# Layer 2's down projection as seven block products of half-size operands

## The reference, cut to what matters

```
D_MODEL, SEQ, D_FF, CONV_W = 1024, 512, 2816, 3
v = rmsnorm(h, norm_ffn_w[l])
gate = causal_depthwise_conv_2(v @ w_gate[l], conv_w[l], conv_b[l])
h = h + (jax.nn.silu(gate) * (v @ w_up[l])) @ w_down[l]
...
return rmsnorm(h, final_norm_w)
```

## Time and profile before

| what | value |
|---|---|
| time, median of 3 runs | 1179.99 us (1179.94 to 1180.92) |
| the profiled execution | 1179.95 us, its span 1178.2 us |
| granted clock of the matrix engine, mean | 0.997 |
| matrix engine busy | 1149.7 us (98%) |
| VectorE, ScalarE, GpSimd busy | 827.9, 628.5, 619.5 us |

### The profile page before, as it was taken

The page is one execution under the profiler, slowest core; times in us unless marked ns, Lnnn a source line. Parts: engine busy times, 40 slices in busy tenths (PEclk is TensorE's granted clock), DMA queues, the critical chain, the costliest instruction groups (busy, mean ns, idle before and its releaser), DMA issues.

```text
span 1178.2 us, 19195 instructions
## 1 busy us (share of the span) xinstructions
PE 1149.7 (98%) x7668; PEld 995.2 (84%) x7668; DVE 827.9 (70%) x1095; ACT 628.5 (53%) x1007; POOL 619.5 (53%) x316
## 2 busy tenths in 40 slices
PE   7999999989999999999999999999999999999997
PEld 6877767779999999888877777778799999998886
DVE  5998974388888887544665577943868888875444
ACT  6346585545666565322455646656556565653323
POOL 3651132696767675544783210018867675755443
PEclk9999999999999999999999999999999999999999
DMA  5688771735866767636432211213245354442221
GB/s 185 236 224 220 191 210 19 187 105 199 202 205 200 200 217 216 196 130 159 118 109 80 72 37 38 74 36 108 74 123 145 110 148 121 144 142 81 100 90 72
DMA packets 110786, 162.64 MB, mean 138 GB/s; under 512 B 3587, under 2 KB 90986, under 8 KB 110698
## 3 DMA queue, kind: packets, MB, share of 16 engines
q1 hardware_dynamic: 97738, 115.02, 30.7%
q0 software_dynamic: 12800, 46.14, 15.9%
q10 hardware_dynamic: 160, 0.26, 0.1%
HBM read 159.05 MB, written 48.23 MB: 176 GB/s over the span
## 4 chain that ended last, share of the span: by engine, by line
PE 86%; DVE 6%; POOL 3%; ACT 3%; issue 1%; DMA 0%; POOLq 0%; ACTq 0%; DVEq 0%
PE ps L2374 34%; PE ps L2425 10%; PE ps L2429 10%; PE ps L2040 6%; PE ps L2041 6%; PE ps L2042 6%; PE ps L2129 4%; PE ps L2613 4%; PE ps L2175 1%; POOL htmp L717 1%; PE ps L2565 1%; PE ps L2160 1%; POOL w_lo L662 1%; DVE diag L1395 1%; DVE act_t L1585 1%
## 5 line engine op out<-in xcount | busy, mean ns | idle before, releaser
L662 POOL TENSOR_TENSOR w_lo<-w_raw,w_hi 128x1024 fp32r<-128x1024 f32 x176 | 458.9, 2624 | 246.5 <-ACT w_hi L806 245.1
L806 ACT ACTIVATE w_hi<-w_raw 128x1024 fp32r<-128x1024 f32 x210 | 220.9, 1054 | 198.3 <-PE ps L2429 77.2
L2374 PE MATMUL ps<-tt,w_hi 128*128 128x256 f32 x1280 | 232.4, 283 | 0.5 <-DVE w_lo L1368 0.3
L2374 PEld LDWEIGHTS ps<-tt,w_hi 128*128 128x128 f32 x1280 | 199.6, 192 | 0.9 <-DVE w_lo L1368 0.5
L2374 PE MATMUL ps<-tt,w_lo 128*128 128x256 f32 x640 | 181.1, 283 | 0.0
L1614 DVE TENSOR_TENSOR tt<-act_t,tt 128x512 fp32r<-128x512 f32 x44 | 99.1, 2259 | 101.7 <-ACT tt L1033 101.7
L2040 PE MATMUL ps<-h_hi,w_hi 128*128 128x512 f32 x376 | 153.0, 407 | 2.4 <-POOL w_lo L662 0.8
L2041 PE MATMUL ps<-h_lo,w_hi 128*128 128x512 f32 x376 | 147.0, 391 | 0.0
L2042 PE MATMUL ps<-h_hi,w_lo 128*128 128x512 f32 x376 | 146.8, 391 | 0.0
L2374 PE MATMUL ps<-h_hi,w_hi 128*128 128x256 f32 x440 | 124.6, 283 | 0.2 <-POOL w_lo L662 0.2
L2374 PE MATMUL ps<-h_lo,w_hi 128*128 128x256 f32 x440 | 124.5, 283 | 0.0
(11 more groups left out here) (334 smaller groups left out, 2284.8 us busy)
## 6 DMA issues: line engine op xcount, KB each, us to landing
blocks<-in_w_up POOLq DMA_DIRECT2D x28, 1408.0 KB, 10.5
w_raw<-in_w_up SPq DMA_DIRECT2D x40, 512.0 KB, 3.6
w_raw<-blocks SPq DMA_DIRECT2D x40, 512.0 KB, 4.0
w_raw<-in_w_in SPq DMA_DIRECT2D x19, 1024.0 KB, 5.4
w_raw<-in_w_down SPq DMA_DIRECT2D x18, 1024.0 KB, 5.0
w_raw<-in_w_gate SPq DMA_DIRECT2D x20, 512.0 KB, 3.7
w_raw<-in_w_out SPq DMA_DIRECT2D x8, 1024.0 KB, 5.2
blocks<-in_w_gate POOLq DMA_DIRECT2D x4, 1408.0 KB, 7.3
```

The costliest lines, as they stand in the source:

```text
L662: pool.tensor_tensor(unit_view(w_lo, at, flat), unit_raw(at, flat), unit_view(w_hi, at, flat).bitcast(F32), ALU.subtract).then_inc(s_lo, 1)
L806: act.activation(unit_view(w_hi, at, flat), unit_raw(at, flat), ACT.Copy).then_inc(s_hi, 1)
L2374: mm = pe.matmul(ps[:, bank, 0:NH], weight[:, k, n], a, start=begin, stop=False, skip_group_check=True)
```

## The change

The activation (transposed, inner dimension by tokens) is cut into 2 x 2 blocks of 1408 x 256, and `w_down_2` into blocks of 1408 x 512. Seven products of sums of blocks take the place of eight products of blocks. A product is a phase (`PHASES = 7`): 11 slices k of 128 rows, two token tiles, three matmuls. A phase has six units (`PHASE_UNITS = 6`): five of 128x1024 (two slices of 512 columns) and one of 128x512. There are now 42 units, and each is loaded on its own.

- **Weights.** Two phases read `w_down_2` alone, four read sums from the new DRAM tensor `dsums`, one reads `w_down_2` again. GpSimd issues 16 more DMAs (`down_sums`): eight copies and eight that add, 704x512 values each (four of the copies are within `dsums`), six during layer 2's input projection and ten in its up projection.
- **Low parts of weights.** From the fifth unit on, VectorE makes four of the six of a phase, GpSimd the first and the fourth.
- **Activation.** The sums of activation blocks (`operand_sum`) are made by VectorE in place in `act_t`, for phases 2, 3, 5 and 6, one step ahead. `operand_hi` and `operand_lo` split each operand, one phase ahead of its use.
- **Results.** Phases 3, 4 and 5 add to what a bank already holds. VectorE adds or subtracts the two banks of a finished phase to the residual in the first two steps of the next phase (`added`).
- **The end.** Token tiles finish in the order 2, 3, 0, 1, and the last phase runs its last three slices tile by tile.

The core of the diff:

```diff
+PHASES, PHASE_UNITS = 7, 6
+U_END = U_DOWN2 + PHASES * PHASE_UNITS
+D_ROW, D_CROSS, D_SUM = (2, 3), (4, 5), (0, 1)
+PHASE_BANK = (D_ROW, D_CROSS, D_SUM, D_ROW, D_SUM, D_ROW, D_CROSS)
+PHASE_FREE = {3: 1, 4: 5, 5: 7, 6: 3}
+TILE_ORDER = (2, 3, 0, 1)
...
 def on_vector(u):
     at = block_of(u)
+    if u >= U_DOWN2 + 4:
+        return (u - U_DOWN2) % PHASE_UNITS not in (0, 3)
...
+SUMS_AFTER |= {u: 1 for u in range(U_IN2 + 5, U_IN2 + 17, 2)}
+SUMS_AFTER |= {u: 1 for u in range(FIRST_BLOCK[1], U_DOWN2, NB)}
...
+            def phases():
+
+                w, k1, k2 = w_down_2[0], slice(0, KP * P), slice(KP * P, DFF)
+                left, right = slice(0, DK), slice(DK, DM)
+                streams = (w[k1, left], w[k2, left], dsums[0], dsums[1], dsums[3], dsums[2], w[k2, right])
+                for p, block in enumerate(streams):
+                    if 2 <= p < 6:
+                        sp.wait_ge(s_prep, 16 * (2 * STEPS + 4 * (p - 1)))
+                    for q in range(PHASE_UNITS):
+                        one_block(U_DOWN2 + PHASE_UNITS * p + q, block[2 * q * P:min(2 * q + 2, KP) * P, :])
...
+            def down_sums(step):
...
+                pool.wait_ge(s_prep, 16 * (2 * STEPS + step))
+                if kind == 0:
+                    pool.dma_start(dsums[to, r, :], begin).then_inc(s_prep, 16)
+                else:
+                    pool.dma_start(dsums[to, r, :], added, accum_op=ALU.add).then_inc(s_prep, 16)
...
+            def phases():
+
+                operand_hi(0, 4)
+                operand_hi(0, 5)
+                for s in range(PHASES * PHASE_UNITS):
+                    p, q = divmod(s, PHASE_UNITS)
+                    if p + 1 < PHASES:
+                        operand_hi(p + 1, q)
+                    if U_DOWN2 + s + 4 < U_END:
+                        lead(U_DOWN2 + s + 4)
...
+            def operand_lo(p, q):
+                dve.wait_ge(s_ahi, KF + PHASE_UNITS * p + q + 1)
+                hi, lo = operand_chunk(p, q)
+                dve.tensor_tensor(lo, operand_source(p, q), hi.bitcast(F32), ALU.subtract).then_inc(s_alo, 1)
+
+            def operand_sum(p, q):
+
+                r11, r12, r21, r22 = (act_block(k0, right, q) for k0 in (0, KP) for right in (0, 1))
+                if p == 2:
+                    dve.wait_ge(s_alo, KF + q + 1)
+                    dve.tensor_tensor(r11, r11, r12, ALU.subtract).then_inc(s_dt, 1)
+                if p == 3:
+                    dve.wait_ge(s_dt, q + 1)
+                    dve.wait_ge(s_alo, KF + 2 * PHASE_UNITS + q + 1)
+                    dve.scalar_tensor_tensor(r11, r22, -1.0, r11, ALU.mult, ALU.subtract).then_inc(s_dt, 1)
+                if p == 5:
+                    dve.tensor_tensor(r12, r22, r12, ALU.subtract).then_inc(s_dt, 1)
+                if p == 6:
+                    dve.wait_ge(s_dt, PHASE_UNITS + q + 1)
+                    dve.wait_ge(s_alo, KF + 3 * PHASE_UNITS + q + 1)
+                    dve.scalar_tensor_tensor(r11, r21, -1.0, r11, ALU.mult, ALU.subtract).then_inc(s_dt, 1)
...
+            for q in range(2, PHASE_UNITS):
+                operand_lo(0, q)
+            dve.wait_ge(s_tc, 8)
+            for s in range(PHASES * PHASE_UNITS):
+                p, q = divmod(s, PHASE_UNITS)
+                low = U_DOWN2 + s + 3
+                if low < U_END and on_vector(low):
+                    rest(low)
+                later, first = divmod(s + 1, PHASE_UNITS)
+                if later + 1 < PHASES:
+                    operand_sum(later + 1, first)
+                if p + 1 < PHASES:
+                    operand_lo(p + 1, q)
+                if p and q < 2:
+                    added(p - 1, q)
...
-            down(1, U_DOWN2)
+            def phase_slice(p, k, t, first):
+
+                u = U_DOWN2 + PHASE_UNITS * p + k // 2
+                n = slice((k % 2) * DK, (k % 2) * DK + DK)
+                whi, wlo = (unit_view(w, u, True)[:, n] for w in (w_hi, w_lo))
+                hi, lo = (o[:, k % 2, t * P:(t + 1) * P] for o in operand_chunk(p, k // 2))
+                bank = PHASE_BANK[p][t]
+                pe.matmul(ps[:, bank, :], hi, whi, start=first, stop=False, skip_group_check=True)
+                pe.matmul(ps[:, bank, :], lo, whi, start=False, stop=False, skip_group_check=True)
+                return pe.matmul(ps[:, bank, :], hi, wlo, start=False, stop=False, skip_group_check=True)
+
+            def phase_ready(p, q):
+
+                wait_lo(pe, U_DOWN2 + PHASE_UNITS * p + q)
+                pe.wait_ge(s_alo, KF + PHASE_UNITS * p + q + 1)
```

230 lines of the change are left out of this document (171 added, 59 removed).

## The result

The changed kernel takes 1182.33 us in the median (1180.59 to 1188.83, 20 runs) where the kernel before takes 1179.99 (1178.93 to 1181.43, 20 runs). The ratio is 1.0021, 95% interval 1.0014 to 1.0027: slower by 0.2%, which is clear of no change and at the edge of what this kernel's measurements can tell. The forecast was 1167.3 us, range 1164.2 to 1174.0. It was wrong, in sign too.

What follows compares the result with a forecast made beforehand. The prediction took the matrix engine, busy 98% of the span, as the bound. From 1179.95 us it took 14.96 (matmuls) and 0.39 (the end) and added 2.7 (VectorE's waits): 1167.3 us, range 1164.2 to 1174.0.

Steps and rivals of the forecast that it cites:

- The matmuls: Layer 2's down projection: 66 fewer matmuls, the rest still at 0.2267 us each, so 14.96 us less.
- Rival D: Down projection: no gain, since matmuls go at another pace with two banks taking turns; about 1180 us, chance 0.02.
- The end: Final norm: the last tile's other half is ready earlier, rest of the final chain the same; 0.39 us off.
- The DMAs for `dsums`: Layer 2's input and up projections: GpSimd's 16 more DMAs cost 0, bounded by 0 and 1 us.
- Rival C: Down projection: the load ring is late, loads taking 9.3 us; slower than before at 1196.5 us, chance 0.07.
- ScalarE and the loads in the stage: Down projection: ScalarE keeps pace, 1.67 of 2.72 us a step; loads hidden with 3.8 us left.
- VectorE with GpSimd: Down projection: excluding each other, they need 16.8 us against a phase's 14.96 in phases 1, 2, 4, 5; 2.7 us lost.
- the fair reading: Down projection: VectorE and GpSimd wait for each other in turn; 2.7 us lost, ends 0.7 and 3.9 us.
- rival B: Down projection: VectorE with GpSimd becomes the bound, each instruction 0.05 us dearer, 4.8 us longer; 1172.1 us, chance 0.26.

Runs made afterwards that it cites:

- e1: Changed kernel, with VectorE making all low parts of weights from the down projection's fifth unit on, GpSimd none: 1170.95 us, ratio 0.9911.
- e4: Changed kernel, all low parts from the fifth unit on VectorE and the input projection's six DMAs after units 9, 11, 13, 15 and 17 (two): 1167.46 us.
- e8: Changed kernel with a small ScalarE copy ahead of each high part whose low part is GpSimd's, from phase 2 on: 1183.55 us, ratio 1.0021.
- e2: Changed kernel, with VectorE waiting in each step for its own last operand split to finish, which leaves gaps: 1177.45 us, ratio 0.9971.
- e3: Changed kernel, the input projection's six DMAs four units later, the last in the output projection: 1181.61 us, ratio 1.0007.

## Why the prediction was wrong, step by step

**The matmuls: right.** 461 distances in 104.94 us where nobody waits (e1 and e4) are 0.2276 us each, and without the 0.38 us that phase 0 loses to VectorE's late splits 0.2268, against 0.2267 forecast. Rival D fell: two banks in turn cost nothing. The saving of 14.96 us is real in every run.

**The end: wrong, small.** The last addition does stand closer to the last matmul (1171.50 - 1171.00 = 0.50 us, before 0.81), as argued. But from the last scaling's start to the end of the span it is now 1179.0 - 1174.29 = 4.71 us, and was 1178.2 - 1174.16 = 4.04. The forecast took that part as unchanged. Together +0.38 instead of -0.39. Most of it is the last store: from its issue to its landing it takes 3.16 us, before 2.71, and 3.14 to 3.16 us in the five other traces with the changed order of token tiles (e1 to e4 and e8). Why is open.

**The DMAs for `dsums`: mis-sized, 2.5 us instead of 0 to 1.** The up projection was judged rightly: it had a pair of rows with and without such DMAs, and they cost nothing there. For the input projection no such pair existed, and I looked only at what is queued behind them on GpSimd. The cost came another way, by a 1024 KB load that landed late. Rival C knew that mechanism (1024 KB at 9.3 us) and put it only in the changed stage. Of the 3.07 us by which the stage begins later, the wait at 623.62 is 2.5: the matmul ahead of it starts at 620.79, before at 620.23, and the one behind it at 623.62, before at 620.55. The other 0.56 us were there ahead of the first such DMA, and are not its doing.

**ScalarE and the loads in the stage: right for the cause.** No wait of the matrix engine's stands behind either. ScalarE did wait 7.8 us for a load of `dsums`, but that load's buffer was the one that the 8.26 us low part held, so it followed from the stall; in e1, without the stall, no such wait stands.

**VectorE with GpSimd: the step that failed.** It rests on one sentence: "Since the two exclude each other, GpSimd's two subtractions ... come on top". That takes for granted that GpSimd's turn comes, and late only by the instruction in front of it; the earlier trace rows shows a single VectorE instruction against a single one of GpSimd's, each with free time around it, and says nothing of a row of VectorE instructions without a gap. The exclusion didn't make VectorE late by 2.41 us, it made GpSimd late by up to 5.9. The accounts had the warning in them: 16.8 us of work in a phase of 14.96 means a VectorE that never stands still. The place was wrong with it: waits behind VectorE's low parts in phases 2 and 5 and none in 3 and 6 were forecast, and the two that came stand behind GpSimd's, at the start of 3 and 6. What followed was 8.6 us of waits and 3.2 us of half clock, where I had 2.7 in all. The half clock was in no step. The sum with the measured terms: -14.96 + 8.6 + 3.2 + 0.5 (phase 0 and small ones) + 2.5 (DMAs) + 0.56 (ahead of them) + 0.38 = +0.8 us, the difference of the two spans.

**Whether the fair reading's size was right stays open.** With GpSimd let in at once (e2) the stage loses 5.2 us, twice my 2.7 and above its end of 3.9. But up to 3.4 us of that is the estimated price of the gaps that let GpSimd in. What is left for fair turns lies between 1.8 and 5.2 us, so this run neither confirms 2.7 nor the 7.5 us of rival B.

**What I didn't try on paper.** By the same prices, all low parts on VectorE are 12.0 + 2 x 1.13 = 14.3 us a phase with sums, under 14.96, with nothing of GpSimd's on top. Giving a third of the work to GpSimd made the sum larger, not smaller. The run e1 bears this out.

## What to carry to other kernels

When two engines exclude each other, add up both their work before sharing a task between them: the second engine shortens nothing, and if the first is then never idle, the second may get its turn only when the first has to wait. Don't price a new transfer by the queue that issues it alone; look at which load it runs beside, and who waits for that load. And count a stall of some 4 us on the matrix engine as longer than it is, here by 1.6 us each.

## What the runs showed of the hardware

**GpSimd kept out until VectorE has nothing ready.** From all fourteen traces I took every subtraction of GpSimd's in the down projection that became ready while VectorE was running without a gap:

| GpSimd's pause before | VectorE without a gap before | cases | VectorE's instructions that went ahead |
|---|---|---|---|
| up to 3.26 us | 0.1 to 88 us | over 50 | none or one in all |
| 3.98 to 6.73 us | 1.6 us or less | 15 | none in all |
| 3.84 to 6.89 us | 5.0 us or more | 32 | two to 39 in 31, none in one |

The second row is mostly e2, where VectorE's last gap of 35 ns lay at most 1.6 us back. So both seem to be needed: GpSimd has done nothing for nearly 4 us, and VectorE has run through that time.

When GpSimd did get in can be read too. In 26 of the 31 it was at VectorE's next gap. In three (1146.20 and its like in e3 and e8) it was beside an addition to the residual, which has one of its inputs in PSUM. In the other two, 1095.44 and its like in e3, no gap shows, but VectorE's next instruction waited for ScalarE, as read above; the wait was met 0.06 us after GpSimd began. The single case of the third row in which none went ahead (a pause of 5.07 us, in the shifted changed kernel) is of the same kind: VectorE's next instruction waited for a high part of ScalarE's that was ready 0.04 us after GpSimd began. So in all 32 GpSimd came in where VectorE had no instruction with two SBUF inputs ready to go. That is read from the traces, not made by an experiment, and how the chip decides is open. What is shown by an experiment is the pause: with it eight of eight and eight of eight stayed out, without it, beside the same instructions, ten of ten got in. And e2 shows the gap.

**Half clock behind a wait.** All six waits of 4.1 us or more in the changed kernel, e3 and e8 were followed, at once or 1.1 us later, by matmuls 0.427 us apart instead of 0.227, for 3 to 5 us; so was the 12.7 us wait. Shorter waits alone don't tell. Of two equal waits of 2.45 and 2.47 us, one was followed by none, the other by some 6 us of it. A wait of 2.8 us at about 258 us stands in all fourteen traces, and half clock goes with it in ten of them; with one of 1.9 us at about 840 us it goes in four, the kernel before among them. So two executions of the same code can differ by it, and a difference of a microsecond or two between single traces is not the kernel's until the stretches at half clock are taken out.
